# Second mixer: the modulation's weight tiles in two staging places and summed earlier, the convolution's first tap on ScalarE, the values' weight sums spread over more quarters

## The reference, cut to what matters

```python
mod = cs @ ada_w[i] + ada_b[i]                       # cs = silu(c); six vectors of 1024
sh1, sc1, g1, sh2, sc2, g2 = split(mod)
h = rms_norm(x, norm_mix_g[i]) * (1 + sc1) + sh1
x = x + g1 * hybrid_mixer_2(h, ...)                  # layer 0
h = rms_norm(x, norm_ffn_g[i]) * (1 + sc2) + sh2     # needs g1, sh2, sc2, g2 only now
x = x + g2 * swiglu(h, ...)

def hybrid_mixer_2(h, w_in, conv_w, conv_b, ...):
    z, xbc, dt_raw, q, k, v = split(h @ w_in)
    xbc = silu(causal_depthwise_conv(xbc, conv_w, conv_b))   # 4 taps per channel
    xs, bm, cm = split(xbc)
    y = ssd_chunked(xs, softplus(dt_raw + dt_bias), ...)
    att = dilated_attention(q, k, v, rel_table)
    return concat([rms_norm(...y * silu(z)...), att]) @ w_out
```

## Time and profile before

| | |
|---|---|
| three runs | 1461.82, 1463.28, 1464.57 us; median 1463.28 |
| the profiled execution | 1465.13 us, its span 1463.4 us |
| PE's granted clock | 0.976 of 2.4 GHz over the span, 1.00 from 484 us to the mixer's end |
| the mixer | PE's first work in it at 477.05 us, the first projection matmul at 485.99 us |

### The profile page before, as it was taken

How to read it: one execution, slowest core, us unless ns; L and a number is a source line. 1 busy time by engine, 2 the same in 40 slices (tenths; PEclk the granted TensorE clock), 3 DMA queues, 4 the chain that set the end, 5 groups by cost and what they waited for, 6 DMA issues and landing times. The chain is left out here.

```text
span 1463.4 us, 18944 instructions
## 1 busy us (share of the span) xinstructions
PE 1376.3 (94%) x7517; PEld 1015.5 (69%) x7517; DVE 870.7 (60%) x1464; ACT 275.6 (19%) x602; POOL 265.6 (18%) x342
## 2 busy tenths in 40 slices
PE   5999999896776999999999999999999999999997
PEld 1877655653442788768888888777766878888843
DVE  2458775432232668753454685788783874777864
ACT  2222221000000311643345101000002113211101
POOL 5078010000000300553355402100020100000000
PEclk9999999998888999999999999999999999999999
DMA  9976887899999697866774455898854552555431
GB/s 350 310 263 226 285 329 298 348 417 415 416 418 385 191 305 261 306 194 162 159 180 133 160 162 176 327 333 322 297 210 150 155 156 73 163 168 172 170 129 47
DMA packets 176057, 355.58 MB, mean 243 GB/s; under 512 B 7289, under 2 KB 137041, under 8 KB 158561
## 3 DMA queue, kind: packets, MB, share of 16 engines
q1 hardware_dynamic: 166720, 313.64, 60.4%
q0 software_dynamic: 9248, 40.71, 9.5%
HBM read 352.58 MB, written 1.74 MB: 242 GB/s over the span
## 5 line engine op out<-in xcount | busy, mean ns | idle before, releaser
L1846 PE MATMUL PS<-HT,ring 128*128 128x256 f32 x1152 | 258.3, 382 | 0.1
L1846 PEld LDWEIGHTS PS<-HT,ring 128*128 128x128 f32 x1152 | 215.5, 190 | 36.0 <-issue 7.9
L1542 DVE TENSOR_TENSOR X<-X,PS 128x1024 f32<-128x1024 f32 x14 | 17.1, 1222 | 113.2 <-PE PS L1318 113.2
L1265 PE MATMUL PS<-ring_extra,slot_rows 128*32 128x256 f32 x576 | 56.3, 450 | 27.6 <-DMA ring_extra<-in_expert_w_gate 7.1
L2876 PE MATMUL PS<-HT,ring 128*128 128x256 f32 x352 | 76.8, 379 | 0.0
L2905 PE MATMUL PS<-ada_stage,half_sums 128*128 128x256 f32 x320 | 75.6, 379 | 0.0
L2905 PE MATMUL PS<-ring,half_sums 128*128 128x256 f32 x320 | 75.6, 379 | 0.0
L2876 PEld LDWEIGHTS PS<-HT,ring 128*128 128x128 f32 x352 | 66.7, 190 | 9.0
L2882 PE MATMUL PS<-ring,hid 128*128 128x512 f32 x160 | 71.8, 592 | 0.0
L2905 PE MATMUL PS<-ring,HT 128*128 128x256 f32 x304 | 68.8, 379 | 0.0
L2905 PEld LDWEIGHTS PS<-ring,half_sums 128*128 128x128 f32 x320 | 59.4, 190 | 11.2 <-issue 4.3
(11 more groups left out here) (736 smaller groups left out, 2465.4 us busy)
## 6 DMA issues: line engine op xcount, KB each, us to landing
ring<-in_hy_w_in SPq DMA_DIRECT2D x40, 1024.0 KB, 8.4
ring_extra<-in_w_ada SPq DMA_DIRECT2D x24, 1024.0 KB, 7.9
ada_stage<-in_ada_w POOLq DMA_DIRECT2D x24, 1024.0 KB, 7.3
ring<-in_ffn_w_gate SPq DMA_DIRECT2D x22, 1024.0 KB, 5.9
ring<-in_ffn_w_up SPq DMA_DIRECT2D x22, 1024.0 KB, 5.8
ring<-in_ffn_w_down SPq DMA_DIRECT2D x22, 1024.0 KB, 5.8
ring_extra<-in_expert_w_down SPq DMA_DIRECT2D x18, 1024.0 KB, 22.9
ring_extra<-in_expert_w_up SPq DMA_DIRECT2D x18, 1024.0 KB, 20.1
```

Of the source, the lines that this page charges most:

```text
L1265: mm = pe.matmul(PS[e * SLOTS:(e + 1) * SLOTS, 2, j * CW:(j + 1) * CW], hs[:, k, e * SLOTS:(e + 1) * SLOTS], w[e][:, k, :], start=(k == 0) ...
L1542: dve.tensor_tensor(part, part, PS[:, 6:8, :], ALU.add).then_inc(added, 1)
L1846: mm = pe.matmul(dst, w[:, k, half * P:(half + 1) * P], HT[:, k, :], start=(k == 0), stop=(k == KT - 1))
```

## The change

The 16 adds move forward: the first in quarter (1, 3), several steps with two, the last in (13, 3). Their tiles go alternately to `stage` and to the first two thirds of `out_sum0` (tile `out_sums`), each with a semaphore of its own, and SP waits for the add two before instead of the one before. The first two loads wait for nothing and are now ahead of the ring loads of the mixer's first step. Tap 0 moves from DVE to ACT, as an Identity activation with scale and bias, just behind the copy of the chunk. The eight weight sums of the values are moved over other quarters, and the first waits for all adds because it writes over a staging place. The load of `gate_a` moves on POOL from behind `small_loads` to quarter (2, 0) and shares their semaphore.

```diff
-        add_at = {(s, 3): s - 2 for s in range(2, 18)}
+        SECOND_ADDS = [(1, 3), (2, 3), (3, 0), (3, 3), (4, 0), (4, 3), (5, 3), (6, 3), (7, 0)] + [(s, 3) for s in range(7, 14)]
+        add_at = {at: a for a, at in enumerate(SECOND_ADDS)}
+        second_stage = (stage[:], out_sum0[:, 0:2].rearrange("p a k n -> p (a k n)"))
-        v_sum_at = {(14, 3): (0, 0), (15, 1): (0, 1), (15, 2): (0, 2), (15, 3): (0, 3),
-                    (16, 1): (1, 0), (17, 2): (1, 1), (17, 3): (1, 2), (18, 1): (1, 3)}
+        v_sum_at = {(14, 3): (0, 0), (15, 3): (0, 1), (16, 1): (0, 2), (16, 2): (0, 3),
+                    (17, 0): (1, 0), (17, 3): (1, 1), (18, 0): (1, 2), (18, 2): (1, 3)}
...
                 for s in range(NP + 12):
-                    for (step_no, _), a in add_at.items():
-                        if step_no == s + (s > 0) or (s == 0 and step_no <= 1):
-                            if a:
-                                sp.wait_ge(summed, a)
-                            sp.dma_start(stage[:].rearrange("p (a n) -> p a n", a=1), wv[:, ds(a // 2, 1), 1 + a % 2, :])\
-                                .then_inc(fetched, 16)
+                    for a in range(ADDS):
+                        if s == (0 if a < 2 else SECOND_ADDS[a - 2][0]):
+                            if a > 1:
+                                sp.wait_ge(summed, a - 1)
+                            sp.dma_start(second_stage[a % 2], wv[:, a // 2, 1 + a % 2, :]).then_inc(fetched[a % 2], 16)
                     send_until(sp, base + s + 1)
...
+                def tap(s):
+                    if s == 0:
+                        act.wait_ge(padded, 1)
+                        act.wait_ge(moved1, 2)
+                    act.wait_ge(evac, s + 1)
+                    for m in range(2):
+                        tile = 2 * XORDER[s] + m
+                        act.activation(conv_tiles(s)[:, m, :], RX[:, s % 3, m, 0:S], ACT.Identity, scale=convT[:, tile:tile + 1],
+                                       bias=convT[:, CONV * XT + tile:CONV * XT + tile + 1]).then_inc(first_tap, 1)
...
+                    if q == (1 if s == 1 else 0) and 1 <= s <= NX:
+                        tap(s - 1)
...
-                    for j in range(CONV):
+                    for j in range(1, CONV):
...
+                            if j == 1:
+                                dve.wait_ge(first_tap, 2 * s + m + 1)
...
+                        if pair == 0:
+                            dve.wait_ge(summed, ADDS)
...
-                pool.dma_start(gate_a[:], t["ada_b"][0][2 * D:3 * D].partition_broadcast(P)).then_inc(late, 16)
                 for s, q in QUARTERS:
                     if (s, q) == (2, 0):
                         pool.wait_ge(moved1, 2)
                         pool.dma_start(bias_dram, bias_rows).then_inc(stored, 16)
+                        pool.wait_ge(small, SMALLS)
+                        pool.dma_start(gate_a[:], t["ada_b"][0][2 * D:3 * D].partition_broadcast(P)).then_inc(small, 16)
```

More of the change, by code:

```diff
@@ L1704, in _program @@
             sem("g_left"), sem("g_right"))
-        late, padded = pool_dma_sem("a_late"), sem("h_padded")
+        padded = sem("h_padded")
         x_squared, x_out = sem("g_xsquared"), sem("o_xout")
@@ L1800, in _program @@
         cv_ok, fetched, summed, cols, cols_ok, rows_a, rows_b, gate_ok = (
-            sem("d_c"), sem("d_fetched"), sem("d_summed"), sem("d_cols"),
+            sem("d_c"), (sem("d_fetched0"), sem("d_fetched1")), sem("d_summed"), sem("d_cols"),
             sem("d_colsok"), sem("d_rows_a"), sem("d_rows_b"), sem("d_gates"))
@@ L1804, in _program @@
         v_summed, v_products, v_moved, v_joined = sem("v_sums"), sem("v_products"), sem("v_moved"), sem("v_joined")
+        first_tap = sem("h_first_tap")
         ADDS = 2 * KT
@@ L2358, in convolve @@
                     dve.wait_ge(evac, s + 1)
-                    if s == 0:
-                        dve.wait_ge(padded, 1)
-                    for j in range(CONV):
+                    for j in range(1, CONV):
                         for m in range(2):
@@ L2365, in convolve @@
                             a = conv_tiles(s)[:, m, :]
-                            if j == 0:
-                                ins = dve.tensor_scalar(a, RX[:, s % 3, m, 0:S], w,
-                                                        convT[:, CONV * XT + tile:CONV * XT + tile + 1], ALU.mult, ALU.add)
-                            else:
[L2370 to L2374, removed]
+                            if j == 1:
+                                dve.wait_ge(first_tap, 2 * s + m + 1)
+                            else:
+                                dve.wait_ge(conv_tap, (CONV - 1) * 2 * s + 2 * (j - 2) + m + 1)
+                            dve.scalar_tensor_tensor(out=a, in0=RX[:, s % 3, m, j:j + S], scalar=w, in1=a,
+                                                     op0=ALU.mult, op1=ALU.add).then_inc(conv_tap, 1)
+                    dve.wait_ge(conv_tap, (s + 1) * 2 * (CONV - 1))
                     dve.sem_inc(conv, 1)
@@ L2391, in add @@
                     j, k = a % 2, a // 2
-                    dve.wait_ge(fetched, 16 * (a + 1))
+                    dve.wait_ge(fetched[j], 16 * (k + 1))
                     if a == 0:
@@ L2395, in add @@
                     if k == 0:
-                        dve.tensor_scalar(acc[:, j, :], stage[:], cv[:, 0:1], None, ALU.mult).then_inc(summed, 1)
+                        dve.tensor_scalar(acc[:, j, :], second_stage[j], cv[:, 0:1], None, ALU.mult).then_inc(summed, 1)
                     else:
                         dve.wait_ge(summed, a - 1)
-                        dve.scalar_tensor_tensor(out=acc[:, j, :], in0=stage[:], scalar=cv[:, k:k + 1], in1=acc[:, j, :],
+                        dve.scalar_tensor_tensor(out=acc[:, j, :], in0=second_stage[j], scalar=cv[:, k:k + 1], in1=acc[:, j, :],
                                                  op0=ALU.mult, op1=ALU.add).then_inc(summed, 1)
@@ L2505, in _ @@
                         dve.wait_ge(rows_a, 1)
-                        dve.wait_ge(late, 16)
+                        dve.wait_ge(small, SMALLS + 16)
                         dve.tensor_tensor(gate_a[:], gate_a[:], PS[:, 2:4, :].rearrange("p a b -> p (a b)"), ALU.add)\
```

## The result

| | median | lowest to highest | runs |
|---|---|---|---|
| before | 1462.55 us | 1460.27 to 1464.57 | 6 |
| after | 1469.06 us | 1464.38 to 1471.17 | 6 |

The ratio after to before is 1.0042, interval 1.0027 to 1.0057: slower by 6.1 us, between 3.9 and 8.3. The forecast of 1463.6 us (1460.4 to 1467.2) missed it.

What follows compares the result with a forecast made beforehand. PE, busy 94% of the span, was taken as the bound. Terms -1.4 (values' waits) + 2.2 (small loads beside tiles) - 0.5 (`gate_a`) = +0.3 us gave 1463.6 us, range 1460.4 to 1467.2 us.

Steps and rivals of the forecast that it cites:

- Part 1: Values' steps of the mixer: moving the adds out removes PE's two waits behind DVE, -1.4 us.
- Both waits: PE's two waits on DVE in the values, at a `move_y` and the first join, together 1.4 us.
- the order that I walked: DVE's new instruction list with measured durations: `move_y` 1 ends near 608.4 us, the first join near 615 us.
- Part 2: Mixer's start: two early 1 MB tiles delay the small loads by 0 to 3.8 us, taken as +2.2 us.
- the quiet stretch: 484.0 to 489.3 us, DMA at 18 GB/s before the change; the two tiles were to fill it.
- What delays the small loads delays PE one for one: PE's `setup` at the mixer's start: no slack, since `quarter_sum` lands just when PE comes; today's wait 0.2 us.
- Part 3: Mixer's start: loading `gate_a` after `setup` frees `quarter_sum`, gain 0 to 1.1 us, taken as 0.5 us.
- Part 4: Convolutions: tap 0 on ACT and adds pulled forward cost nothing; `convolve(3)` done at 529 us, 8 us of cover left.
- A longer stop at the start: Rival, mixer's start: small loads held for two stops of 3.8 us, 1469.5 us; decides from 4.3 us added wait; chance 0.14.
- No delay at the start: Rival, mixer's start: small loads pass between the tiles, `gate_a` being away makes up the rest; 1461.7 us; chance 0.28.

Runs made afterwards that it cites:

- the first profile: Profile of the changed kernel against the kernel before, from the fastest of its six runs: 1464.38 us; median of the six 1469.06 us, ratio 1.0042.
- the second: The changed kernel run again with no edit, for another profile: profiled execution 1474.49 us, median 1469.04 us, ratio 1.0043 to the kernel before.
- the converse: Kernel before, with its first modulation tile and an unused 1 MB load issued at the mixer's start, all else unchanged: ratio 1.0063 to the kernel before.

## Why the prediction was wrong

**Part 1, the values, held.** Both waits went, by D 1.37 us of the 1.4 reckoned. Two things behind it did not hold: the new quarters of the sums have no part in it, and in the kernel with early tiles the waits went with the adds in place, so the order that I walked is not all that decides the collision.

**Part 2, "how much later is `ada_c`", is the step that failed.** The place and the chain of it were right: the tiles fill the quiet stretch (260 GB/s, where I had expected some 350), POOL goes on some 0.4 us after `ada_c`'s landing (486.85 - 479.03 - 7.4 = 0.42 us in the rows above, and about as much in each other profile), `quarter_sum` is late, PE waits. The sum had +2.2 us for it; what stands in its place is 1.5 + 3.3 = 4.8 us in the first profile and 5.3 + 5.4 = 10.7 us in the second. Three things in it were off.

1. The delay was 4.1 us, 4.3 to 4.4 in later profiles, not 2.2, and above the 3.8 that I had called its upper bound. That bound was one landing beside traffic taken as the longest there can be. The forecast's sentence on the Trainium skill, page "DMA: Bandwidth & Descriptors", section "Queues, rings and completion order", put one turn at an estimated 3.2 us; the measurements lie above it too, in its direction, and no run shows a turn. Per tile the delay was 2.3 and then 2 us more.
2. I counted this delay once. A `quarter_sum` that is late can meet the ring load of chunk 6, and then takes 6.3 us instead of 3.7. That, and PE's start that came 1.0 us sooner, made the wait 5.3 us in one profile and 1.5 in the other.
3. "What delays the small loads delays PE one for one" was wrong. With the wait the clock was at half for 6.8 to 13.7 us. B and C grew by 3.3 us in the first profile and by 5.4 in the second. My sum had no term for it, though it was larger than the wait in one profile and as large in the other.

With these the sum closes: for the first profile -1.4 + 1.5 + 3.3 = +3.4 us (+3.5 in the table, unrounded), for the second -1.4 + 5.3 + 5.4 = +9.3 us. The measured +6.1 us [3.9, 8.3] lies between the two. In the first profile, the rest of the 4.45 us that the stretch took is 1.0 us ahead of A, between PE's first work in the mixer and its first projection matmul, where the profiles vary between 8.8 and 9.95 us, kernels with early and with late tiles alike. Of these terms the wait with what it entails was tested by delaying the tiles and by the converse, the clock's part by the 28 matmuls, the ring load's by holding it.

**Part 3, `gate_a`, is small, and its size stays open.** I had let 0.5 us count. `quarter_sum` landed in 3.5 to 3.7 us in the kernels with late tiles, against 4.7 before. This difference of up to 1.2 us isn't `gate_a`'s alone: before, the ring load went out at 493.17 us, 1.4 us ahead of `quarter_sum`'s landing, and no run moved `gate_a` alone. With late tiles PE hardly feels it: A is 8.7 us as before, and B 3.2 to 3.3 us. In the converse experiment, where `gate_a` stayed in its place, `quarter_sum` took 6.6 us against 6.2 to 6.3 without it, so some 0.3 us beside the tiles.

**Part 4 held.** From the cumulation to `products` each kernel takes the same 8.46 us, with no wait. The last convolution that `products` needs ended at 526.35 + 2.46 = 528.8 us, where I had 529. Tap 0 costs 593 ns on ACT instead of the 500 that I took from a different activation, and is hidden as reckoned. That one takes its scale as a number (`scale=-1.0`), where tap 0 reads it from a column of `convT` as it does its bias. DVE's and ACT's rows after:

```profile
526.35 2.46 DVE L2382 SCALAR_TENSOR_TENSOR b_c<-rx_zb,conv_T,b_c 128x256 f32<-128x256 f32 x6
```

```profile
L2149 ACT ACTIVATE y_T<-rx_zb,conv_T 128x256 f32<-128x256 f32 x16 | 8.7, 593 | 0.3
```

**The rivals.** "A longer stop at the start", chance 0.14, named the place, the side and the point from which it decides, 4.3 us of added cost. That its 1469.5 us comes close to the measured 1469.06 is luck: its price of 3.8 us twice was the wrong make-up, since there was one longer stop, a second encounter with a load in only some executions, and the clock. "No delay at the start" fell.

**Open.** Why the half clock lasts 6.8, 10.2 or 13.7 us in different executions. Why POOL's stop ends with a landing: it was so in every profile, but no run changed the number of loads in front. How often `quarter_sum` meets the ring load: two profiles of the changed kernel show one of each, and all three of the other kernels in which it could. Whether the values' waits of before occur in each of its executions. What varies ahead of the mixer, where PE's first work in it begins between 469.69 and 477.52 us.

## What to carry to other kernels

A wait that is just met, here by 0.2 us, deserves the most careful part of a forecast. Ask what else delays the thing waited for, what it meets once it is late, and what TensorE's clock does behind the wait; here the clock cost as much as the wait. A transfer that looks free because the queue is quiet can still hold up small loads that the next step needs: order it behind them, which here cost nothing and kept the gain. Compare one profile with another by stretches between fixed instructions, since the span alone hid the loss here.

## What the runs showed of the hardware that was not expected

- The clock. A wait of 1.3 us, with `setup`'s short matmuls behind it, was followed, 2.3 us after its end, by 6.8 us at 1.2 GHz; a remaining wait of 0.7 to 1.1 us left it at 2.4 GHz, and so did 28 matmuls in place of a 6 us wait. Ten matmuls and then 3.08 us of idling did not.
- Small loads beside large ones. `ada_c`, 4 KB, landed after 2.7 to 3.3 us on a quiet queue, 5.6 beside one tile of 1 MB, 7.4 to 7.7 beside two.
- POOL's stop among its small loads at the mixer's start lasted from 2.50 to 7.45 us and each time ended some 0.45 us after the landing of the load ahead of it.
